# The first norm of a two-block network on one core: normalised by token and turned, with the early loads and half a modulation block placed elsewhere

## What is computed

```python
cond = jax.nn.silu(c)
mod = (cond @ ada_w[i] + ada_b[i])[:, None, :]
sh1, sc1, g1, sh2, sc2, g2 = jnp.split(mod, 6, axis=-1)
h = rmsnorm(x, norm1_g[i]) * (1.0 + sc1) + sh1
...
qkv = h @ w_qkv                      # rmsnorm: x * rsqrt(mean(x * x) + EPS) * gain
```

## Time and profile before

| what | value |
|---|---|
| runs, median (lowest to highest) | 1005.11 us (1004.39 to 1007.44) |
| the profiled execution, its time | 1006.84 us |
| its span in the trace | 1005.1 us |
| PE busy | 948.1 us, 94% |
| DVE busy | 815.8 us, 81% |
| ACT busy | 510.4 us, 51% |
| POOL busy | 32.7 us, 3% |
| mean DMA rate | 231 GB/s |

### The profile page before, as it was taken

The page is one execution under the profiler, slowest core; times in us unless marked ns, Lnnn a source line. Parts: engine busy times, 40 slices in busy tenths (PEclk is TensorE's granted clock), DMA queues, the critical chain, the costliest instruction groups (busy, mean ns, idle before and its releaser), DMA issues.

```text
span 1005.1 us, 19223 instructions
## 1 busy us (share of the span) xinstructions
PE 948.1 (94%) x7511; PEld 909.6 (91%) x7511; DVE 815.8 (81%) x1204; ACT 510.4 (51%) x799; POOL 32.7 (3%) x48
## 2 busy tenths in 40 slices
PE   3598879999999999999999999999999899999997
PEld 2597469999999999988999999999999899999996
DVE  6886887899859999787699976999997699985732
ACT  3243975555433366554764542337677555543423
POOL 3000000000000010000000000003000000000000
PEclk9998879999999999999999999999999999999998
DMA  8972378499929997664159992998724349992901
GB/s 299 382 261 105 126 236 268 134 315 323 302 98 369 363 342 260 208 224 161 56 172 320 295 362 86 381 349 258 235 65 135 118 162 306 327 321 82 379 13 43
DMA packets 144416, 232.20 MB, mean 231 GB/s; under 512 B 6249, under 2 KB 75409, under 8 KB 144353
## 3 DMA queue, kind: packets, MB, share of 16 engines
q1 hardware_dynamic: 142993, 228.75, 66.2%
q0 software_dynamic: 1072, 2.05, 0.9%
q10 hardware_dynamic: 288, 0.54, 0.2%
HBM read 230.27 MB, written 1.05 MB: 230 GB/s over the span
## 4 chain that ended last, share of the span: by engine, by line
PE 74%; DVE 16%; DMA 4%; issue 3%; ACT 1%; SPq 1%; DVEq 0%; ACTq 0%
PE M L1602 18%; PE M L1604 17%; PE M L1603 17%; DVE ACC L1009 8%; DVE WL L986 3%; PE AUX L1756 2%; DMA ADA<-in_ada_w 2%; DMA RAW<-in_ada_w 1%; PE AUX L2156 1%; PE M L1620 1%; PE M L1622 1%; DMA RAW<-in_wqkv_a 1%; PE M L1626 1%; PE AUX L1669 1%; PE M L1674 1%
## 5 line engine op out<-in xcount | busy, mean ns | idle before, releaser
L599 ACT ACTIVATE WH<-RAW 128x2048 fp32r<-128x2048 f32 x136 | 258.9, 1913 | 228.2 <-PE M L1604 73.6
L1602 PE MATMUL M<-XH,WH 128*128 128x256 f32 x1264 | 363.5, 288 | 5.4 <-DVE XL L1563 3.1
L1603 PE MATMUL M<-XL,WH 128*128 128x256 f32 x1264 | 359.9, 285 | 0.0
L1604 PE MATMUL M<-XH,WL 128*128 128x256 f32 x1264 | 359.9, 285 | 0.0
L986 DVE TENSOR_TENSOR WL<-RAW,WH 128x2048 fp32r<-128x2048 f32 x136 | 309.6, 2285 | 42.8 <-ACT WH L599 42.5
L1602 PEld LDWEIGHTS M<-XH,WH 128*128 128x128 f32 x1264 | 244.8, 194 | 7.5 <-issue 3.5
L1603 PEld LDWEIGHTS M<-XL,WH 128*128 128x128 f32 x1264 | 244.8, 194 | 0.3
L1604 PEld LDWEIGHTS M<-XH,WL 128*128 128x128 f32 x1264 | 244.9, 194 | 0.0
L1009 DVE SCALAR_TENSOR_TENSOR ACC<-ADA,COND,ACC 128x512 f32<-128x512 f32 x266 | 199.9, 751 | 9.2
L1602 PE MATMUL M<-MH,WH 128*128 (+1 forms) x528 | 149.2, 283 | 3.3 <-DVE WL L986 3.2
L1603 PE MATMUL M<-ML,WH 128*128 (+1 forms) x528 | 148.0, 280 | 0.0
(11 more groups left out here) (274 smaller groups left out, 1314.3 us busy)
## 6 DMA issues: line engine op xcount, KB each, us to landing
ADA<-in_ada_w SPq DMA_DIRECT2D x68, 1024.0 KB, 5.4
RAW<-in_w_gate SPq DMA_DIRECT2D x44, 512.0 KB, 6.2
RAW<-in_w_up SPq DMA_DIRECT2D x44, 512.0 KB, 7.3
RAW<-in_w_down SPq DMA_DIRECT2D x44, 512.0 KB, 7.4
RAW<-in_w_ffn_in SPq DMA_DIRECT2D x44, 512.0 KB, 6.9
RAW<-in_wqkv_b SPq DMA_DIRECT2D x24, 512.0 KB, 5.2
RAW<-in_w_ffn_out SPq DMA_DIRECT2D x22, 512.0 KB, 7.1
RAW<-in_w_in SPq DMA_DIRECT2D x16, 512.0 KB, 7.7
```

Source lines behind the costliest of these rows:

```text
L599: act.activation(WH[:, s, :], RAW[:, s, :], ACT.Copy).then_inc(h_ready, 1)
L1602: pe.matmul(out_ap, wh, xh, start=start, stop=False, skip_group_check=True)
L1603: pe.matmul(out_ap, wh, xl, start=False, stop=False, skip_group_check=True)
L1604: return pe.matmul(out_ap, wl, xh, start=False, stop=stop, skip_group_check=True)
```

## The change

1. **Loads.** The eight row DMAs leave SP's queue; ACT asks for them after it has made COND. CONST is loaded in two parts: the identity and eight columns first, the rest by ACT after the rows. x is asked for after block 1, not after block 0. POOL waits for the last half of block 3, not for x.
2. **Norm by token.** ACT squares XTOK as it lies, 128 tokens x 1024, with the sum taken along (XSUM), takes the root of it, copies the turned x to X as before, and then multiplies XTOK by RSTD into XN_TOK (which lies in PR and PT). PE turns that (16 transposes, into six tiles of M and two of AUX), ACT copies it to TMP. Token means, POOL's sums and the spread of the root fall away for this norm. DVE computes QA = TMP x coefficient + shift, ACT computes XH from TMP in the same way, and DVE XL = QA - XH.
3. **Block 3.** Its first four tiles are multiplied on PE (`ada_direct`: 16 matmuls of one column, with the weight itself as the stationary operand), its last four on DVE; both add up in the same columns of AUX. a_chain counts four less from there on (`summed`).
4. **K/V weight.** It is taken in two halves of 1024 elements, each with its own semaphore: `kv_half` on ACT, `kv_low` on DVE, the second half between tiles of the norm. PE waits for the second half only at the fifth tile.
5. **Biases.** Three blocks are added at once, behind the loads of the rows.

The core of the diff:

```diff
+        XN_TOK = [rows[:, :, :, :].rearrange("p a e n -> p (a e n)")[:, 0:D] for rows in (PR, PT)]
+        XN = [M[:, 2 + j, :] for j in range(6)] + [AUX[:, j, :] for j in range(2)]
...
+        def summed(b, kt):
+            return KT * b + kt - (KT // 2 if b >= 3 else 0)
...
-            load_rows(sp, EARLY_ROWS, early_rows_in)
...
-                if b == 0:
+                if b == 1:
...
-                             qkv_a_src[:, 4 * q:4 * q + 4, D:D + 256]).then_inc(landed[0], 16)
+                             qkv_a_src[:, 4 * q:4 * q + 4, D:D + 256]).then_inc(kv_landed[q], 16)
...
-            pool.wait_ge(x_in, 16)
+            pool.wait_ge(early_landed[3][1], 16)
...
-            for n in range(5):
+            for n in range(1, 5):
...
-            act.dma_start(CONST[:, :], a["kept"]).then_inc(const_in, 16)
+            act.dma_start(CONST[:, 0:KEPT_EARLY], a["kept"][:, 0:KEPT_EARLY]).then_inc(const_in, 16)
...
+            load_rows(act, EARLY_ROWS, early_rows_in)
+            act.dma_start(CONST[:, KEPT_EARLY:K_W], a["kept"][:, KEPT_EARLY:K_W]).then_inc(rest_in, 16)
...
-            act.wait_ge(rows_turned, 1)
-            columns(EARLY_ROWS)
...
+            act.wait_ge(ang_v, 10)
+            act.activation(SIN[:, :], ANG[:, 0, :], ACT.Sin).then_inc(ang_s, 1)
+            act.activation(COS[:, :], ANG[:, 1, :], ACT.Sin, bias=cc(C_HALFPI)).then_inc(ang_s, 1)
+            act.preload_act_table(ACT.Sqrt)
+            act.wait_ge(x_in, 16)
+            for m in range(2):
+                act.activation(XN_TOK[m], XTOK[:, m, :], ACT.Square, accum_out=XSUM[:, m:m + 1]).then_inc(sq_ready, KT // 2)
+            act.wait_ge(sq_ready, KT)
+            act.activation(STD[:, :], XSUM[:, :], ACT.Sqrt, scale=1.0 / D, bias=cc(C_EPS)).then_inc(std_ready, 1)
             for j in range(KT):
                 act.wait_ge(x_turned, j // 2 + 1)
                 act.activation(X[:, j, :], M[:, j, :], ACT.Copy).then_inc(x_ready, 1)
-
-            act.wait_ge(ang_v, 10)
-            act.activation(SIN[:, :], ANG[:, 0, :], ACT.Sin).then_inc(ang_s, 1)
-            act.activation(COS[:, :], ANG[:, 1, :], ACT.Sin, bias=cc(C_HALFPI)).then_inc(ang_s, 1)
-            norm(0, before=lambda: high(U0["qkv_a"], 0))
+            act.wait_ge(rstd_ready, 1)
+            for m in range(2):
+                act.activation(XN_TOK[m], XTOK[:, m, :], ACT.Copy, scale=RSTD[:, m:m + 1]).then_inc(xn_ready, 1)
+            def kv_half(h, ready):
+                act.wait_ge(kv_landed[h], 16)
+                at = slice(1024 * h, 1024 * h + 1024)
+                act.activation(WH[:, 0, at], RAW[:, 0, at], ACT.Copy).then_inc(ready, 1)
+            for j in range(KT):
+                act.wait_ge(xn_turned, j // 2 + 1)
+                act.activation(TMP[:, j, :], XN[j], ACT.Copy).then_inc(t_ready, 1)
+            kv_half(0, kv_high)
+            act.wait_ge(rows_turned, 1)
+            columns(EARLY_ROWS)
+            act.wait_ge(t_ready, KT)
+            act.wait_ge(coef_ready, 1)
+            for j in range(KT):
+                act.activation(XH[:, j, :], TMP[:, j, :], ACT.Identity, scale=COEF[:, j:j + 1], bias=mod(0, 0, j)).then_inc(hh_ready, 1)
+                if j == 1:
+                    kv_half(1, h_ready)
...
+                        first = kt == (4 if b == 3 else 0)
...
+            def early_bias():
+                dve.wait_ge(vc_ready, len(EARLY_ROWS))
+                dve.wait_ge(acc_red, 3)
+                dve.tensor_tensor(MOD[:, 0:12], ADP[:, 0:12], VC[:, 0:12], ALU.add).then_inc(mod_ready, 3)
+                dve.wait_ge(acc_red, 4)
+                dve.tensor_tensor(MOD[:, 12:16], AUX[:, 4, 0:4], VC[:, 12:16], ALU.add).then_inc(mod_ready, 1)
...
-            dve.wait_ge(vc_ready, len(EARLY_ROWS))
-            for b in range(1, 4):
-                ada_sum(b, 0)
-                ada_bias(b - 1)
-            low(U0["qkv_a"], 0)
-            ada_bias(3)
-
+            ada_sum(1, 0)
+            root(0)
+            ada_sum(2, 0)
             dve.wait_ge(ang_s, 2)
             dve.tensor_scalar(COS[:, :], COS[:, :], cc(C_ROPE), cc(C_KEEP), ALU.mult, ALU.add).then_inc(trig_ready, 1)
+            ada_sum(3, 0, rows=range(4, 8))
+            def kv_low(h, high_ready, ready):
+                dve.wait_ge(high_ready, 1)
+                at = slice(1024 * h, 1024 * h + 1024)
+                dve.tensor_tensor(WL[:, 0, at], RAW[:, 0, at], WH[:, 0, at], ALU.subtract).then_inc(ready, 1)
+            def first_row(j):
+                dve.tensor_scalar(QA[:, j, :], TMP[:, j, :], COEF[:, j:j + 1], mod(0, 0, j), ALU.mult, ALU.add).then_inc(xv_ready, 1)
+            def first_low(j):
+                dve.wait_ge(xv_ready, j + 1)
+                dve.wait_ge(hh_ready, j + 1)
+                dve.tensor_tensor(XL[:, j, :], QA[:, j, :], XH[:, j, :], ALU.subtract).then_inc(xin_ready, 1)
+            kv_low(0, kv_high, kv_low_ready)
+            early_bias()
+            coefficients(0)
+            dve.wait_ge(t_ready, KT)
+            dve.wait_ge(coef_ready, 1)
+            for j in range(KT + 1):
+                if j < KT:
+                    first_row(j)
+                if j == 4:
+                    kv_low(1, h_ready, l_ready)
+                if j >= 1:
+                    first_low(j - 1)
...
-            norm(0)
...
+                at = 4 * b if b < 3 else 0
...
-            pe.wait_ge(early_rows_in, 16 * row_dmas(EARLY_ROWS))
-            turn_rows(EARLY_ROWS)
+            ada_reduce(0)
             pe.wait_ge(x_in, 16)
             for j in range(KT):
                 for m in range(2):
                     mm = pe.transpose(M[:, j, m * P:(m + 1) * P], XTOK[:, m, j * P:(j + 1) * P], IDENT)
                 if j % 2 == 1:
                     mm.then_inc(x_turned, 1)
-            ada_reduce(0)
-            norm(0, blocks=range(1, 4))
+            ada_reduce(1)
+            pe.wait_ge(x_ready, KT)
+            for m in range(2):
+                pe.wait_ge(xn_ready, m + 1)
+                for j in range(KT):
+                    mm = pe.transpose(XN[j][:, m * P:(m + 1) * P], XN_TOK[m][:, j * P:(j + 1) * P], IDENT)
+                    if m == 1 and j % 2 == 1:
+                        mm.then_inc(xn_turned, 1)
+            def ada_direct(kts):
+                for kt in kts:
+                    for j in range(4):
+                        pe.matmul(AUX[:, 4, j:j + 1], EARLY[3][:, kt, j * P:(j + 1) * P], COND[:, kt:kt + 1],
+                                  start=kt == 0 and j == 0, stop=False, skip_group_check=True)
+            pe.wait_ge(cond_ready, 1)
+            pe.wait_ge(early_landed[3][0], 16)
+            ada_direct(range(0, 2))
+            ada_reduce(2)
+            ada_direct(range(2, 4))
+            pe.wait_ge(early_rows_in, 16 * row_dmas(EARLY_ROWS))
+            turn_rows(EARLY_ROWS)
+            pe.wait_ge(a_chain, summed(3, KT))
+            for j in range(4):
+                mm = pe.matmul(AUX[:, 4, j:j + 1], ACC[:, acc_slot(3), j * P:(j + 1) * P], cc(C_ONE), start=False, stop=True,
+                               skip_group_check=True)
+            mm.then_inc(acc_red, 1)
...
-            pe.wait_ge(l_ready, base + 1)
+            pe.wait_ge(rest_in, 16)
+            pe.wait_ge(kv_low_ready, 1)
             for kt in range(KT):
+                if kt == KT // 2:
+                    pe.wait_ge(l_ready, 1)
```

64 lines of the change are left out of this document (36 added, 28 removed).

## The result

The changed kernel takes 1002.32 us (median of 14 runs, 998.37 to 1007.61) against 1006.39 (14 runs) of the kernel before on the same chip: 4.1 us less. The ratio measured over all these runs is 0.9945, 95% interval 0.9926 to 0.9965, which is 5.5 us (3.5 to 7.4) of 1006.39; it is not the quotient of the medians, 0.9960. 1000.9 had been forecast, 4.2 us less than a first median of 1005.11, a ratio of 0.9958. The profiled execution took 1004.96 us, its span is 1002.9.

What follows compares the result with a forecast made beforehand. The body was taken as TensorE-bound, the head as bound by serial chains; the start of WL of unit 1 moves from 51.84 to 47.6, so 4.2 us off 1005.11 gives 1000.9 us. Range 998.0 to 1005.5.

Steps and rivals of the forecast that it cites:

- first MB landed: Head, transfers: first MB of modulation weights lands at 6.65 us, from 9.5 less the 2.85 of earlier asking.
- x there, first square: Head: x, now the fifth MB, lands at 19.2 us, 4.5 later than before; ACT's squares start then.
- direct products, two reductions, rows: PE, head: 32 direct records at 0.213 us (6.8), reductions of blocks 2 and 3, row turns; 10.8 us in all.
- DVE waits for block 3's half until; sum done: DVE, head: the fourth block's second half lands at 30.0 us; its four products end at 33.0.
- mark: Start of DVE's WL of unit 1, where steady pace begins: from 51.84 us to 47.6, a gain of 4.2.
- the chain through x: Head: x, ACT's squares, root, copies and scalings, PE's turns, direct products and reductions end last; coefficients at 40.5 us.
- the cover over block 3, K/V and POOL's loads: Head: fourth block ready 5.4 us ahead of 38.45; K/V landed by 36.5 at latest, even with POOL's loads costing 3.8.
- The bound of 20.5 for x: Head: latest landing of x allowed for, in us, at which the gain would be 2.9 us.
- rival 3: PE, head: the clock rises in the new chain, records take half of 0.213 us; gain 7.7, total 997.4; chance 0.08.
- the forecast's own range: Whole kernel: 999.2 to 1002.7 us, from x landing at 18.0 or 20.5 (gain 5.4 or 2.9) and hand-overs 0.5 either way.
- Rivals 1 and 2: Head: ACT's issues wait for SP's, until 18.3 us (1004.0, chance 0.25) or 2.5 us each (1011.2, chance 0.10).
- Rival 4: Behind the head, 60 to 150 us: slow clock or late blocks swallow some 3 of 4.2 us; 1004; chance 0.11.

## Why the prediction was right

| step | forecast | measured |
|---|---|---|
| first MB landed | 6.65 | 9.9 (1.56 + 8.3) |
| x there, first square | 19.2 | 21.87 |
| nine ACT issues done | by 9 | 7.5 |
| root | 21.7 | 24.4 |
| turned copies done | 24.3 | 26.6 |
| turns of scaled x done | 29.0 | 31.1 |
| direct products, two reductions, rows | 10.8 | 7.6 (10.6 at 1.2 GHz) |
| DVE waits for block 3's half until; sum done | 30.0; 33.0 | 32.65; 35.5 |
| coefficients | 40.5 | 38.88 |
| first matmul | 41.5 | 40.42 |
| mark | 47.6 | 46.29 |

**Right** were the mark as measure, the chain through x as what ends last, the cover over block 3, K/V and POOL's loads (DVE's half was ready 1.4 us ahead of the last reduction), the costs on ACT (squares and root 2.5 us as forecast), and that the gain goes through: 5.55 us at the mark, 4.1 and 5.4 between the medians of two timings. From coefficients to mark 7.1 us were forecast and 7.4 measured.

**Mis-sized, the start of the transfers.** "First MB at 9.5 - 2.85 = 6.65" took the landing time of 5.1 us along with the issue. It was 8.3, and all of x's 2.6 us (and the 2.65 of block 3's half) come from there: from the first MB to x 12.55 us had been forecast and 11.9 were measured. The bound of 20.5 for x was too low. Asking 2.85 us earlier made the first MB 0.4 us **later** (9.9 for 9.5). The runs show the low rate up to 6 us and that ACT's nine loads are 0.6 us of it (9.3 without them); why the rest of the start is slow they don't show.

**Mis-sized, the pace of PE.** "So I price the direct products at 0.213" held in two of the eight profiled executions with direct products (positions on SP's queue, ACT's loads behind the root); in the other six the clock rose, and rival 3, given 0.08, came in half. The argument against it used one-column matmuls alone, 4.4 us of them, which indeed had not raised the clock; but sixteen more turns stood ahead of them here. (Sixteen turns and a reduction, 5.2 us without a pause, raised it neither in the two executions of the kernel before nor from 21.82 on in the changed one, so turns don't always do it.) The Trainium skill (TensorE: Matmul & The Clock Gate, Part 1) was cited for the rise: the trace agrees for the turns and not for the one-column matmuls, between which the clock fell again.

The two sizes nearly cancel, 2.6 late and 3.2 early, and that is luck; 0.5 less for copies and turns and 0.5 less for hand-overs make up the 1.6 us by which the coefficients came earlier than forecast. With the clock low the gain at the mark was 3.0 us in the run with the positions on SP's queue (51.84 - 48.81). With x as late as in the changed kernel it would be about 2.5, an estimate from that run and the 0.6 us between the two x, just above the 2.4 at the lower end of the forecast's own range. So the forecast rests on a size of x that was too small and on a pace that was too slow.

**Rivals 1 and 2** fall: with SP's issue held for 5.49 us, ACT's went out at 0.23 to 0.85 us. The Trainium skill (Perfetto Trace Analysis, DMA Instruction, HWDGE) says the descriptor block is locked for one sequencer until all descriptors of an instruction are generated; the trace does not show that here as far as it concerns an issue that is held by a full queue. **Rival 4** is what one pair of profiles looked like (5.55 at the mark, 2.2 at the end), by stretches at the lower clock, between 760 and 830 us and before, that come in some executions of either kernel.

## What to carry to other kernels

Find one instruction behind which the kernel runs at its steady pace and measure edits of the head there: it repeated within 0.4 us where whole executions differed by 10 (what the clock does behind it is a measurement of its own). A load moved to the front takes with it the start-up of the transfers and every instruction that waits for the load which it overtook: the early weights cost 4.65 us with the old order of the work, while the whole change, of which they are a part, gained 5.55. Before work goes to an idle engine, ask whether that engine stands in the chain that ends last: half a block moved from DVE to PE gained nothing.
